# Interleaving branch segments with softmax-like heads: two large PE blocks in place of four small ones

## The reference

```
z       = q @ k.T * scale                     # scores
log_1m  = where(valid, log_sigmoid(-z), 0)
after   = reverse_cumsum(log_1m) - log_1m
a       = where(valid, exp(log_sigmoid(z) + after), 0)
out     = a @ v                               # then: gated = out * silu(z path)
merged += sigmoid(gate) * (gated @ w_branch)  # per branch
```

## Time and profile before

| what | value |
|---|---|
| median of three runs | 2224.4 us (2224.31 to 2224.58) |
| profiled execution, its own time | 2225.11 us |
| span of that execution, first to last instruction | 2223.3 us |
| PE busy | 2208.7 us, 99% of the span |
| DVE, ACT, POOL busy | 1539.5, 947.2, 234.8 us |
| granted TensorE clock, mean | 0.999 |

### The profile page before, as it was taken

One profiled execution on the slowest core, in us unless ns is written; L12 is line 12 of the kernel. 1 busy time (PEld: TensorE's weight loads), 2 busy tenths in 40 slices (PEclk: granted clock), 3 DMA queues, 4 the chain that ended last, 5 costly groups with the idle time before them and its releaser, 6 DMA issues.

```text
span 2223.3 us, 38578 instructions
## 1 busy us (share of the span) xinstructions
PE 2208.7 (99%) x16186; PEld 2163.9 (97%) x16186; DVE 1539.5 (69%) x1788; ACT 947.2 (43%) x1280; POOL 234.8 (11%) x335
## 2 busy tenths in 40 slices
PE   9999999999999999999999999999999999999998
PEld 7999999999999999999999999999988999999998
DVE  7876768657666667676676666666577577778676
ACT  5343434334444444434444444444555234324543
POOL 0000000000100023323320000000001112100000
PEclk9999999999999999999999999999999999999999
DMA  6444453534444445454545343444765765763448
GB/s 181 116 128 110 111 144 103 150 105 124 122 117 123 131 130 145 122 143 102 142 109 136 108 133 111 129 116 135 236 210 151 250 194 175 189 169 90 130 131 270
DMA packets 426060, 318.04 MB, mean 143 GB/s; under 512 B 13325, under 2 KB 386965, under 8 KB 424480
## 3 DMA queue, kind: packets, MB, share of 16 engines
q1 hardware_dynamic: 403520, 251.18, 41.0%
q0 software_dynamic: 22288, 63.87, 9.2%
q10 hardware_dynamic: 80, 0.52, 0.1%
HBM read 254.53 MB, written 60.99 MB: 142 GB/s over the span
## 4 chain that ended last, share of the span: by engine, by line
PE 96%; DVE 1%; DMA 1%; ACT 1%; issue 0%; POOL 0%; SPq 0%; DVEq 0%; POOLq 0%; ACTq 0%
PE pp L1029 67%; PE pp L1255 12%; PE pp L1431 7%; PE M L1047 2%; PE pp L1039 1%; PE M L1347 1%; PE pp L1528 1%; PE M L1216 1%; PE M L1039 1%; PE M L1368 1%; PE M L1276 1%; PE M L1301 1%; DMA gt_lo<-gated_scratch 1%; PE M L1407 0%; PE pp L1514 0%
## 5 line engine op out<-in xcount | busy, mean ns | idle before, releaser
L1029 PE MATMUL pp<-xa,wa_hi 128*128 128x288 f32 x7392 | 1480.3, 296 | 0.1
L1029 PEld LDWEIGHTS pp<-xa,wa_hi 128*128 128x128 f32 x7392 | 1185.5, 188 | 1.1 <-DVE zs L2170 0.4
L1029 PE MATMUL pp<-xa,wa_lo 128*128 128x288 f32 x3696 | 1086.7, 294 | 0.0
L1029 PEld LDWEIGHTS pp<-xa,wa_lo 128*128 128x128 f32 x3696 | 696.1, 188 | 0.0
L2058 DVE TENSOR_TENSOR wa_lo<-raw_a,wa_hi 128x1024 fp32r<-128x1024 f32 x262 | 319.3, 1221 | 223.5 <-ACT wa_hi L1550 223.4
L1550 ACT ACTIVATE wa_hi<-raw_a 128x1024 fp32r<-128x1024 f32 x262 | 276.7, 1056 | 204.8 <-PE pp L1029 203.8
L2058 DVE TENSOR_TENSOR wa_lo<-raw_r,wa_hi 128x1024 fp32r<-128x1024 f32 x134 | 177.2, 1322 | 147.8 <-ACT wa_hi L1550 147.8
L1550 ACT ACTIVATE wa_hi<-raw_r 128x1024 fp32r<-128x1024 f32 x134 | 141.4, 1055 | 134.0 <-PE pp L1029 126.7
L1255 PE MATMUL pp<-gt_hi,wb_hi 128*128 128x288 f32 x768 | 169.1, 302 | 0.7 <-DMA gt_lo<-gated_scratch 0.7
L1255 PE MATMUL pp<-gt_hi,wb_lo 128*128 128x288 f32 x768 | 164.3, 295 | 0.0
L1255 PE MATMUL pp<-gt_lo,wb_hi 128*128 128x288 f32 x768 | 164.3, 295 | 0.0
(11 more groups left out here) (368 smaller groups left out, 2568.5 us busy)
## 6 DMA issues: line engine op xcount, KB each, us to landing
raw_a<-in_w_in_dram SPq DMA_DIRECT2D x202, 512.0 KB, 5.1
raw_r<-in_w_in_dram SPq DMA_DIRECT2D x68, 512.0 KB, 5.1
z_scratch<-zs POOLq DMA_DIRECT2D x56, 576.0 KB, 3.3
raw_b<-in_w_branch_dram SPq DMA_DIRECT2D x48, 512.0 KB, 4.3
gz<-z_scratch SPq DMA_DIRECT2D x48, 288.0 KB, 4.3
raw_a<-in_w_out_dram SPq DMA_DIRECT2D x20, 512.0 KB, 6.4
gt_hi<-gated_scratch SPq DMA_DIRECT2D x4, 1152.0 KB, 7.4
gt_lo<-gated_scratch SPq DMA_DIRECT2D x4, 1152.0 KB, 10.5
```

Source lines behind the costliest of these rows:

```text
L1029: i = nc.tensor.matmul(out, ws[:, slot, k, :], xa[:, o, part, k, :], start=opens and k == 0 and s == 0, stop=k == HK - 1 and s == 2, skip_ ...
```

## The change

The two inner places in which segments stood between the halves of `scores(i)` and after `weigh_values` are emptied. PE's order in a period was: A, segment, B, segment, transposes of head i-1, segment, values of head i-1, segment (none in the short periods). It becomes: A, B, two segments, transposes, two segments (one in the short periods), values, and then directly the next head's A and B. The tiles come in the same order and each period holds the same number of segments. What frees bank 2 is now a semaphore of its own, `sample_gated`, raised by the first of `gate_head`'s two instructions; the transposes wait for it too, and the wait for all of `g_ready` moves to `weigh_values`. On DVE, merges are moved: those of the first pair stand before `key_weights(i-1)`, those of the second pair after `exponents(i)`. `key_weights(7)` is moved ahead of `split_lo(17)`, and on SP's queue past_v(7) ahead of ml_k.

```
-SB_SLOTS = [[1, 1, 1, 1]] * 3 + [[1, 1, 1, 0]] * 3
+SB_SLOTS = [[2, 2]] * 3 + [[2, 1]] * 3
...
+        sample_gated = sem("sample_gated")
...
+            head_past_v(SBH - 1)
             ml_k_in(0)
-            head_past_v(SBH - 1)
...
-            def scores(i, between=()):
+            def scores(i):
...
                 for qb, col, w in SB_QUERIES:
                     if col >= SB_BANK:
-                        for h, s in between:
-                            seg(h, s)
                         if i >= 2:
-                            pe.wait_ge(g_ready, PG + i - 1)
+                            pe.wait_ge(sample_gated, i - 1)
...
             def weights_to_keys(i):
...
                 if i:
-                    pe.wait_ge(g_ready, PG + i)
+                    pe.wait_ge(sample_gated, i)
...
             def weigh_values(i):
                 pe.wait_ge(at_read, i + 1)
+                if i:
+                    pe.wait_ge(g_ready, PG + i)
...
             for i in range(2, SBH):
-                scores(i, sb_segs(i, 0))
+                scores(i)
+                for h, s in sb_segs(i, 0):
+                    seg(h, s)
+                weights_to_keys(i - 1)
                 for h, s in sb_segs(i, 1):
                     seg(h, s)
-                weights_to_keys(i - 1)
-                for h, s in sb_segs(i, 2):
-                    seg(h, s)
                 weigh_values(i - 1)
-                for h, s in sb_segs(i, 3):
-                    seg(h, s)
...
-                nc.vector.tensor_tensor(z[:, TP:T], M[:, SB_OUT:SB_OUT + TS], z[:, TP:T], ALU.mult)
+                nc.vector.tensor_tensor(z[:, TP:T], M[:, SB_OUT:SB_OUT + TS], z[:, TP:T], ALU.mult
+                                        ).then_inc(sample_gated, 1)
...
                 logits(i)
-                for h in sb_halves(i, 0):
-                    merge(h)
                 gated_lo(PG + i - 2, zsb[i % 2][:, :])
                 above_zero(i)
                 split_lo(At(2 * i + 2))
-                for h in sb_halves(i, 1):
+                for h in sb_halves(i, 0):
                     merge(h)
                 key_weights(i - 1)
                 sums_from(i)
-                for h in sb_halves(i, 2):
-                    merge(h)
                 exponents(i)
-                for h in sb_halves(i, 3):
+                for h in sb_halves(i, 1):
                     merge(h)
             gate_head(SBH - 2)
+            key_weights(SBH - 1)
             split_lo(At(H_SB + 1))
-            key_weights(SBH - 1)
```

## The result

The changed kernel takes 2227.56 us (median of 22 runs, 2225.06 to 2231.19), the kernel before 2224.42 in the same comparison (22 runs, 2222.84 to 2228.13): ratio 1.0014, 95% interval 1.0008 to 1.0020. That is 3.1 us slower, where I said 0.9, and 0.6 us above the top of my range; it lies within the 0.2% that I called no change, though the interval leaves out a ratio of 1. The profiled execution took 2226.64 us with a span of 2224.9.

A forecast was written before the change was run, and what follows sets the result against it. PE bounds it, busy 2208.7 of 2223.3 us. PE's 0.36 gain and past_v's 0.7 become waiting for gt_lo, whose lateness adds 0.9: span 2224.2, median 2225.3 from 2224.4; range 2223.0 to 2227.0.

The forecast's parts named there:

- the falling clock: Rival, end of stage: PE's clock falls in the longer wait, two segments take 6.4 us more, 2231.7; chance 0.04.
- PE's blocks: Head periods on PE: the new block order saves 0.05 us per long and 0.07 per short period, 0.36 in all.
- The rival in which each change of blocks left out saves 0.26 us: PE's periods: nine pairs of block changes go, -2.4 us, 2220.6 with both 0.7 waits gone; chance 0.04.
- Part B's gate: Before part B of the scores: DVE gates the sample in time, cost 0, up to 0.5 us for scores(6).
- its rival: Part B waits for the sample's gating, 1 us for each of heads 2 to 7, 2229.5; chance 0.07.
- merge(13), +0.9: DVE, end of the head stage: merge(13), now behind exponents, starts 0.9 us later, and gt_lo and seg(16,0) with it.
- gt_lo, 19.0 us behind merge(13): End of the head stage: gt_lo lands 19.0 us behind merge(13)'s start, as before the change.
- What stands in front of gt_lo, the same: SP's queue: the transfers ahead of gt_lo stay the same, only past_v and ml_k swapped, so gt_lo is left alone.
- The swap, wait on past_v gone or up to 0.4: SP's queue: past_v ahead of ml_k saves 1.8 us; the 0.7 wait before head 7's values goes or keeps 0.4.
- One wait on gt_lo of 2.2 to 2.6: PE before seg(16,0): its one wait, on gt_lo, grows from 0.7 to 2.2 to 2.6 us.
- From there on no difference: Behind seg(16,0), which starts some 0.9 us later: the rest of the span is unchanged.
- The rival that the landing follows gt_free (0.25): End of stage: gt_lo lands with seg(15,0), 0.36 us earlier or sooner, at most 1.8 us won, 2222.6 to 2224.0; chance 0.25.

The follow-up runs named there:

- e9: Kernel before with merge(13) alone moved behind exponents(7), run for its profile: 2228.02 us, ratio 1.0015 to the kernel before.
- e10: Changed kernel with the swap undone, past_v(7) again behind ml_k on SP's queue: 2228.20 us, ratio 1.0015 to the kernel before.
- e1: Changed kernel with merge(13) alone moved back ahead of exponents(7): 2225.75 us, ratio 1.0007 to the kernel before.
- e8: Kernel before with POOL's product of each mLSTM head held until DVE has summed the squares: 2226.01 us, ratio 1.0006 to the kernel before.
- e5: Changed kernel with POOL's product of each mLSTM head held until DVE has summed the squares: 2228.74 us, ratio 1.0019 to the kernel before.
- e11: Changed kernel run again unaltered for a second profile: 2227.95 us, ratio 1.0016 to the kernel before.
- e4: Kernel before with gz(17) and weights(18) moved on SP's queue behind ml_k and past_v(7): 2222.70 us, ratio 0.9991 to the kernel before.
- e3: Changed kernel with gz(17) and weights(18) moved on SP's queue behind ml_k and past_v(7): 2223.84 us, ratio 0.9999 to the kernel before.
- e6: Changed kernel with gz(17) moved back on SP's queue and POOL's product held until DVE has summed the squares: 2223.82 us, ratio 0.9998 to the kernel before.

## Why the prediction was wrong

The mechanism was right: a late merge(13) holds SP's queue, idle DMA engines start late, and gt_lo lands late. The sum was too small. A rival of 0.04, the falling clock, is seen in e9, e10 and e1, and by the mean clocks in part of the changed kernel's executions too. By its steps:

- **PE's blocks, -0.36 us: wrong, +0.1.** The forecast periods were 19.96 and 16.75, the measured ones 20.03 and 16.83. Parts A and B together take 2.84 us where 1.75 + 1.0 was read. The 0.1 us a period of uncertainty that I had named for B took the whole gain, and with it the 0.29 by which head 7's scores were to come earlier. The rival in which each change of blocks left out saves 0.26 us is out with it.
- **Part B's gate, 0: right**, with 0.2 us to spare. No wait recurs on it. (The price that I gave its rival should read 2229.3: 2225.3 + 6 - 2.)
- **merge(13), +0.9: right mechanism, short by 0.7.** Its absolute start, 1723.90, is near the 1723.7 forecast, but only because this execution reached head 2 half a microsecond earlier. Counted from there it is +1.6: the scans start 0.35 later than forecast (most of it PE's 0.3 that didn't come) and take 0.1 longer than the 3.34 I used, and 0.2 I had taken off for ACT's lag.
- **gt_lo, 19.0 us behind merge(13): right in the first pair (18.97 and 18.96)**, 18.3 and 19.5 in the second, 19.2 (e8) and 18.9 (e5) in the third, 19.8 in e1, 18.4 in e9 and 18.3 in e10. These tenths put another 0.6 on the mean of two pairs and 0.3 on that of three; whether that is the swap, something else of the change or chance is open. In all seg(16,0) starts 2.2 us later in two pairs, 1.9 in three. The executions whose clock stood above 0.998 differ by somewhat more in their medians: 2226.46 to 2226.96 against 2224.1 to 2224.5.
- **What stands in front of gt_lo, the same: right, but its bytes are not all.** From 1723.95 to gt_lo's landing the engines of the kernel before moved 5.8 MB (324 GB/s over 17.8 us), and gt_lo with all that was issued ahead of it, from gz(17) on, is 5.0 MB. Over 0.7 MB issued behind gt_lo went through before it had landed, so the statement that its 11.9 us fit the bytes in front of it does not quite hold.
- **The swap, wait on past_v gone or up to 0.4: wrong.** It stayed at 1.7 and 1.1 us, with the values due at 1733.7 as forecast. I took 1.8 us off past_v's 8.2 for the bytes of ml_k. It lands with what is issued just ahead of it, ml_k before and G_h now, and G_h itself takes 8.5 us in the changed kernel's first profile where it took 7.5. Of the 1.8 us about 1 came.
- **One wait on gt_lo of 2.2 to 2.6: two waits of 1.7 and 1.2, or 1.1 and 2.3.** Together 2.9 and 3.4.
- **From there on no difference: not quite.** The wait at the squares is 0.8 and 0 us in the two profiles before, 1.3 and 1.0 in those after, and the stage behind seg(16,0) is 0.4 us longer in the mean (281.4 against 281.0). The late transfers may bring POOL's product and the sums together; two profiles of each don't show it.
- **The clock, chance 0.04: too low.** I worked from the earlier trace rows, where it falls after about 3 us, and took 2.2 to 2.6 as safe. It fell behind waits of 2.66 (e9), 2.2 (e10) and 1.8 us (e1), held in others of 2.3 (e11 and e1) and 1.7, and is down in 13 of 32 executions of the changed kernel against 14 of 109 before. I put down to it what the median has beyond the 2.3 or so of the landing and the squares, some 0.7 us. At which wait it falls in the changed kernel itself was not seen: both its profiles have it at full speed here.
- **The rival that the landing follows gt_free (0.25): wrong**; the landing keeps its distance to merge(13) to 18.3 to 19.8 us, over both kernels, e1, e9 and e10, where its distance to its own issue goes from 11.2 to 13.9.

The step that failed is the sum of the stage's end: +0.9 for merge(13) and with it for gt_lo and seg(16,0), where merge(13) came 1.6 later and seg(16,0) 2.2 (1.9 over three pairs). What was only argued: that the falls of the clock make up the remaining 0.7 us. The counts go with it: 13 of 32 executions of the changed kernel at 0.998 or below, and 2 of 22 of e3 and e6, where the free queue takes both waits away. But a count is not a sight of the fall (e4's profiled execution is at 0.998 without one), and no kernel here kept PE busy through the wait alone.

## What to carry to other kernels

When a work is moved behind another on one engine, look for the queue that waits for it: here a merge of 0.65 us moved behind exponents of 1.6 left the DMA engines idle that much longer, with a full queue behind the waiting issue. Putting the transfers that don't need the awaited work ahead of the wait was worth more (3 to 4 us put into the changed kernel, 1.8 into the kernel before) than anything in the order of PE's blocks. An interleave that leaves out block changes is only worth what a start-to-start time of the very sequence shows; times of its parts in other company, off by 0.1 us, decided the sign. And a wait that grows from 1 to 2 us on an otherwise full PE should be priced with a clock that may fall to half behind it.

## What the runs showed of the hardware

- The granted clock fell to 0.50 behind waits of 1.8 (e1), 2.2 (e10) and 2.66 us (e9) of a PE otherwise busy, and stayed there for over 8 us in e9 and some 7 us in e10, while PE worked without a gap; behind waits of 1.7 us (after) and 2.3 (e11, e1) it stayed at 1.00.
- Two DVE sums with both inputs in SBUF took 0.83 us alone (e5), 1.02 all but alone (e4) and 2.04 to 3.06 beside POOL's product of 2.65 us, ending 0.7 us behind it wherever they had started.
- A transfer of 64 KB took 8.2 us when issued 0.5 us behind one of 576 KB, and 2.0 (e4) and 3.2 (e3) when issued over 5 us behind it: it landed 0.1 to 0.5 us behind the transfer issued just ahead of it in every profile, whichever that was.
